# Latents and memory queries of an attention layer: from TensorE transposes to VectorE squares and transfers

## The reference, cut to what matters

```python
h = rmsnorm(x, pre_norm_g[l])
z = h @ w_in[l]
q_lat, kv_lat, k_pe, gb, gc, xin, q_mem, gate = split_cols(z)     # 512, 256, 64, ..., 512 columns
q = rmsnorm(q_lat, q_norm_g[l]) @ w_uq[l]                         # the latents, multiplied again
kv = rmsnorm(kv_lat, kv_norm_g[l]) @ w_ukv[l]
sc = einsum('bshd,bmhd->bhsm', q_mem, mk) * MEM_HEAD_DIM ** -0.5  # memory attention
```

## Time and profile before

| | us |
|---|---|
| median of three runs | 2298.61 |
| the profiled execution | 2298.59 |
| its span, first to last instruction | 2296.8 |
| PE busy | 2285.5 |
| DVE busy | 1506.8 |
| ACT busy | 1172.6 |

### The profile page before, as it was taken

The page is one execution under the profiler, slowest core; times in us unless marked ns, Lnnn a source line. Parts: engine busy times, 40 slices in busy tenths (PEclk is TensorE's granted clock), DMA queues, the critical chain, the costliest instruction groups (busy, mean ns, idle before and its releaser), DMA issues.

```text
span 2296.8 us, 27462 instructions
## 1 busy us (share of the span) xinstructions
PE 2285.5 (100%) x10741; PEld 1916.9 (83%) x10741; DVE 1506.8 (66%) x2067; ACT 1172.6 (51%) x1535; POOL 25.5 (1%) x35
## 2 busy tenths in 40 slices
PE   9999999999999999999999999999999999999998
PEld 7888888888888888888888888888888888888887
DVE  6677776756666666676466656675677856576764
ACT  6555655444445744444444444466555456556443
POOL 0000000000000000000000000000000000000000
PEclk9999999999999999999999999999999999999999
DMA  8666665766667566666666666666566665656664
GB/s 294 179 195 201 193 187 169 222 201 203 195 206 267 174 193 198 194 186 200 193 193 193 194 191 207 229 181 188 168 180 176 203 217 149 198 163 182 178 196 137
DMA packets 250129, 446.25 MB, mean 194 GB/s; under 512 B 20784, under 2 KB 55088, under 8 KB 249360
## 3 DMA queue, kind: packets, MB, share of 16 engines
q1 hardware_dynamic: 249568, 443.97, 63.7%
q10 hardware_dynamic: 432, 0.53, 0.1%
HBM read 434.99 MB, written 2.10 MB: 190 GB/s over the span
## 4 chain that ended last, share of the span: by engine, by line
PE 98%; DVE 1%; ACT 1%; DMA 0%; issue 0%; SPq 0%; DVEq 0%; ACTq 0%
PE pm L988 30%; PE pm L990 30%; PE pm L989 30%; PE pb L676 1%; PE pb L858 1%; PE pb L756 1%; DVE wl L2221 0%; PE pb L766 0%; DMA raw<-in_w_in 0%; ACT wh L1494 0%; PE pb L837 0%; PE pb L840 0%; PE pm L983 0%; PE pb L841 0%; PE pm L982 0%; PE pb L839 0%
## 5 line engine op out<-in xcount | busy, mean ns | idle before, releaser
L2221 DVE TENSOR_TENSOR wl<-raw,wh 128x1024 fp32r<-128x1024 f32 (+3 forms) x786 | 947.7, 1210 | 667.3 <-ACT wh L1494 664.0
L1494 ACT ACTIVATE wh<-raw 128x1024 fp32r<-128x1024 f32 (+3 forms) x786 | 819.2, 1046 | 901.3 <-PE pm L990 896.4
L988 PE MATMUL pm<-wh,hTh 128*128 128x512 f32 x702 | 275.2, 392 | 1.0 <-DVE wl L2221 1.0
L989 PE MATMUL pm<-wl,x2Th 128*128 128x512 f32 x704 | 273.9, 389 | 0.0
L990 PE MATMUL pm<-wh,x2Tl 128*128 128x512 f32 x704 | 273.9, 389 | 0.0
L988 PE MATMUL pm<-wh,x2Th 128*128 128x512 f32 x704 | 273.9, 389 | 0.0
L989 PE MATMUL pm<-wl,hTh 128*128 128x512 f32 x702 | 273.3, 389 | 0.0
L990 PE MATMUL pm<-wh,hTl 128*128 128x512 f32 x702 | 273.3, 389 | 0.0
L988 PE MATMUL pm<-wh,xT3h 128*128 128x512 f32 (+1 forms) x640 | 249.1, 389 | 0.0
L990 PE MATMUL pm<-wh,xT3l 128*128 128x512 f32 (+1 forms) x640 | 244.6, 382 | 0.0
L989 PE MATMUL pm<-wl,xT3h 128*128 128x512 f32 (+1 forms) x640 | 244.4, 382 | 0.0
(11 more groups left out here) (427 smaller groups left out, 3223.6 us busy)
## 6 DMA issues: line engine op xcount, KB each, us to landing
raw<-in_w_in SPq DMA_DIRECT2D x286, 512.0 KB, 3.9
raw<-in_w_ffn_gate SPq DMA_DIRECT2D x88, 512.0 KB, 4.3
raw<-in_w_ffn_up SPq DMA_DIRECT2D x88, 512.0 KB, 4.3
raw<-in_w_ffn_down SPq DMA_DIRECT2D x88, 512.0 KB, 4.1
raw<-in_w_o SPq DMA_DIRECT2D x64, 512.0 KB, 4.3
raw<-in_w_in SPq DMA_DIRECT2D x68, 256.0 KB, 3.5
raw<-in_w_branch_b SPq DMA_DIRECT2D x32, 512.0 KB, 4.2
raw<-in_w_out SPq DMA_DIRECT2D x32, 512.0 KB, 4.6
```

The source lines that it names most:

```text
L988: e.matmul(o, ah[:, kk, t], h[:, c], start=first, stop=False)
L989: e.matmul(o, ah[:, kk, t], l[:, c], start=False, stop=False)
L1494: e.activation(h[:, 0:n], r[:, 0:n], ACT.Copy).then_inc(s["hi"], 1)
L2221: e.tensor_tensor(l[:, 0:n], r[:, 0:n], h[:, 0:n].bitcast(F32), ALU.subtract).then_inc(s["lo"], 1)
```

## The change

The order of the first three groups becomes `qm`, `ql`, `kv`; the other groups keep their steps, and L is now the first step of `qm`. The 22 blocks that PE transposed in a layer (8 for `ql`, 4 for `kv`, 2 for the rope key, 8 for `qm`) are transposed as squares by DVE and moved by three batches of 16 transfers, as for `uq`. The two buffers, `latZ` and `latR`, are used by all three batches in turn; `kvZ` and `kvR` are the same memory. The results of round 4 are transposed into a buffer of their own, 12 steps earlier, and the level products of a head and what follows are due one step later.

```diff
+        add(f"qm{l}", "xT3", w_i, 2368, ev=("a", 2))
         add(f"ql{l}", "xT3", w_i, 0, ev=("a", 2))
         add(f"kv{l}", "xT3", w_i, 512, 320, ev=("a", 2))
-        add(f"qm{l}", "xT3", w_i, 2368, ev=("a", 2))
         gt(3)
         uq(0)
...
-RESULTS = ((1, 4, 12, 80, 100), (3, 4, 0, 135, 160), (4, 2, 4, 163, 173))
+RESULTS = ((1, 4, 12, 80, 100), (3, 4, 0, 135, 160), (4, 2, 4, 151, 163))
...
+            L = p.first[f"qm{l}"]
+            for i, (at0, free, value) in enumerate(((19, "c_l", 2 * l), (36, "qm_l", l + 1), (58, "ql_l", 4 * l + 4))):
+                Z, R = (m.kvZ, m.kvR[l]) if i == 2 else (m.latZ, m.latR[l])
+                for n in range(16):
+                    if n % 2 == 0:
+                        yield L + at0 + n // 2
+                    w.wait_ge(s["zl"], 4 * l + i + 1 + (i == 2))
+                    w.wait_ge(s[free], value)
+                    a_, c = n // 4, n % 4
+                    e.dma_start(R[32 * c:32 * c + 32, a_, :, :, :], Z[32 * a_:32 * a_ + 32, c, :, :, :]
+                                ).then_inc(s["d_lat"], 16)
...
-            yield at0 + 22 + i
+            yield at0 + 23 + i
...
-        yield from lat_turns(l, "ql", 2, L + 19)
-        yield from lat_turns(l, "kv", 1, L + 39)
-        yield L + 41
...
-            yield L + 50 + 2 * i
...
+    def latents(l):
...
+        yield p.first[f"qm{l}"] + 73
+        w.wait_ge(s["d_lat"], 768 * l + 768)
+        for k in range(2):
+            e.activation(m.kvT[0][:, k, :].rearrange("p (h a t) -> p h a t", h=2, a=4),
+                         m.kvR[l][:, :, k, :, :].rearrange("p a h t -> p h a t"), ACT.Copy, scale=m.gcol(f"kv{l}", k)
+                         ).then_inc(s["kv_h"], 1)
+        if l:
+            w.wait_ge(s["pv"], 12)
+        e.activation(m.kpeT[0][:, 0, :].rearrange("p (h a t) -> p h a t", h=2, a=4),
+                     m.kvR[l][:, :, 2, :, :].rearrange("p a h t -> p h a t"), ACT.Copy).then_inc(s["kp_c"], 1)
...
+        yield L + 34
+        w.wait_ge(s["d_lat"], 768 * l + 256)
+        e.activation(m.qmT[0][:, :, :].rearrange("p k (h a t) -> p k h a t", h=2, a=4),
+                     m.latR[l][:, :, :, :, :].rearrange("p a k h t -> p k h a t"), ACT.Copy).then_inc(s["qm_c"], 1)
+        yield L + 40
+        w.wait_ge(s["mk_c"], 2 * l + 2)
+        e.activation(m.mkS[0][:, :, :], m.mkT[l][:, :, :], ACT.Copy).then_inc(s["mk_h"], 1)
...
-        yield L + 37
+        yield L + 52
+        for k in range(4):
+            w.wait_ge(s["d_lat"], 768 * l + 512)
+            e.activation(m.qlT[0][:, k, :].rearrange("p (h a t) -> p h a t", h=2, a=4),
+                         m.latR[l][:, :, k, :, :].rearrange("p a h t -> p h a t"), ACT.Copy, scale=m.gcol(f"q{l}", k)
+                         ).then_inc(s["ql_h"], 1)
+        yield L + 54
         w.wait_ge(s["rstd"], RS[f"kv{l}"])
         for half in range(2):
             e.activation(m.S2[1][:, half, 0:256], m.S2[1][:, half, 0:256], ACT.Copy, scale=m.rs[f"kv{l}"][:, half:half + 1]
                          ).then_inc(s["kv_s"], 1)
-        yield L + 40
-        w.wait_ge(s["kv_t"], l + 1)
-        high_gain(6, m.kvT[0], 0, f"kv{l}", 0, "kv_h")
-        w.wait_ge(s["mk_c"], 2 * l + 2)
-        e.activation(m.mkS[0][:, :, :], m.mkT[l][:, :, :], ACT.Copy).then_inc(s["mk_h"], 1)
-        yield L + 42
-        w.wait_ge(s["kp_t"], l + 1)
-        if l:
-            w.wait_ge(s["pv"], 12)
-        e.activation(m.kpeT[0][:, :, :], view(7, 1), ACT.Copy).then_inc(s["kp_c"], 1)
-        yield p.end[f"qm{l}"]
-        w.wait_ge(s["ql_t"], 2 * l + 2)
-        w.wait_ge(s["sq"], SQ[f"ql{l}"])
-        taken(0, f"qm{l}", m.S2[0], scale=f"r{r}")
-        for i in range(2):
-            yield L + 51 + 2 * i
-            w.wait_ge(s["qm_t"], 2 * l + i + 1)
-            e.activation(m.qmT[0][:, 2 * i:2 * i + 2, :], view(6 + i), ACT.Copy).then_inc(s["qm_c"], 1)
...
+            for u in range(3):
+                r, n, k0, at0, split = RESULTS[u]
                 if u == 1:
                     yield from queries(l, (1, 2))
+                src, R = (m.yS4, m.yR4) if u == 2 else (m.yS, m.yR[l])
                 for i in range(16):
                     if u == 0 and i == 12:
                         yield from queries(l, (0,))
+                    if u == 2 and i == 8:
+                        yield from queries(l, (3,))
                     yield L + at0 + (i if n == 4 else i // 2)
                     w.wait_ge(s["ys"], 4 * (6 * l + r + 1))
-                    w.wait_ge(s["y_l"], 5 * l + u)
+                    w.wait_ge(s["y_l"], 5 * l + min(u, 1))
                     a, c = i // 4, i % 4
...
                 ins.then_inc(s["yq"], 1)
-                if u == 1:
-                    yield from queries(l, (3,))
-                yield L + split + 2
-                w.wait_ge(s["y_h"], 5 * l + (1, 2, 5)[u])
-                e.tensor_tensor(m.yT[1][:, k0:k0 + n, :], m.yR[l][:, 0:n, :], m.yT[0][:, k0:k0 + n, :].bitcast(F32),
-                                ALU.subtract).then_inc(s["y_l"], 1)
+                if u == 0:
+                    yield from results_low(l, 0)
+            yield from results_low(l, 1)
+            yield from results_low(l, 2)
...
-        w.wait_ge(s["kv_t"], l + 1)
+        w.wait_ge(s["d_lat"], 768 * l + 768)
...
+    def group_squares(S, n):
...
+        Z = m.latZ if n == 4 else m.kvZ
+        e.transpose(Z[:, :, 0:n, :, :].rearrange("p r k h t -> p k h r t"),
+                    S[:, :, 0:128 * n].rearrange("p h (k r c) -> p k h r c", k=n, r=4)).then_inc(s["zl"], 1)
+    def low_carried(dst, k, R, gname, after, value):
...
+        w.wait_ge(s["d_gain"], 16)
+        w.wait_ge(s[after], value)
+        for half in range(2):
+            hi, lo = (x[:, k, half * 128:half * 128 + 128].rearrange("p (a t) -> p a t", a=4) for x in dst)
+            ins = e.scalar_tensor_tensor(lo, R[:, :, k, half, :], m.gcol(gname, k), hi.bitcast(F32), ALU.mult, ALU.subtract)
+        return ins
...
     def layer(l):
-        L = p.first[f"ql{l}"]
+        L = p.first[f"qm{l}"]
+        yield p.end[f"qm{l}"] + 1
+        w.wait_ge(s["ev_a"], p.evac[f"qm{l}"])
+        w.wait_ge(s["xt_l"], 16 * l + 32)
+        group_squares(m.S2[0], 4)
         yield p.end[f"ql{l}"]
         variance(f"ql{l}", 512, SQ[f"ql{l}"], False)
-        for i in range(2):
-            yield L + 20 + i
-            low_gain(6 + i, m.qlT, 2 * i, f"q{l}", 2 * i, "ql_h", 4 * l + 2 * i + 2, "ql_l")
+        yield L + 34
+        w.wait_ge(s["ev_a"], p.evac[f"ql{l}"])
+        w.wait_ge(s["d_lat"], 768 * l + 256)
+        group_squares(m.S2[0], 4)
+        yield L + 35
+        w.wait_ge(s["qm_c"], l + 1)
+        hi, lo = (x[:, :, :].rearrange("p k (h a t) -> p k h a t", h=2, a=4) for x in m.qmT)
+        e.tensor_tensor(lo, m.latR[l][:, :, :, :, :].rearrange("p a k h t -> p k h a t"), hi.bitcast(F32), ALU.subtract
+                        ).then_inc(s["qm_l"], 1)
+        yield L + 42
+        w.wait_ge(s["mk_h"], l + 1)
+        e.tensor_tensor(m.mkS[1][:, :, :], m.mkT[l][:, :, :], m.mkS[0][:, :, :].bitcast(F32), ALU.subtract
+                        ).then_inc(s["mk_l"], 1)
         yield p.end[f"kv{l}"]
         variance(f"kv{l}", 256, SQ[f"kv{l}"], False)
...
-        yield L + 40
-        low_gain(6, m.kvT, 0, f"kv{l}", 0, "kv_h", 2 * l + 2, "kv_l")
-        w.wait_ge(s["mk_h"], l + 1)
-        e.tensor_tensor(m.mkS[1][:, :, :], m.mkT[l][:, :, :], m.mkS[0][:, :, :].bitcast(F32), ALU.subtract
-                        ).then_inc(s["mk_l"], 1)
-        yield L + 42
-        low(7, m.kpeT, 0, 1, "kp_c", l + 1, "kp_l")
-        for i in range(2):
-            yield L + 51 + 2 * i
-            low(6 + i, m.qmT, 2 * i, 2, "qm_c", 2 * l + i + 1, "qm_l")
+        yield L + 53
+        for k in range(4):
+            low_carried(m.qlT, k, m.latR[l], f"q{l}", "ql_h", 4 * l + k + 1).then_inc(s["ql_l"], 1)
+        yield L + 56
+        w.wait_ge(s["kv_s"], 2 * l + 2)
+        w.wait_ge(s["d_lat"], 768 * l + 512)
+        group_squares(m.S2[1][:, :, 0:256], 2)
+        w.wait_ge(s["rp"], RP[f"kv{l}"])
+        e.transpose(m.kvZ[:, :, 2, :, :].rearrange("p r h t -> p h r t"),
+                    m.kpd[:, :, :].rearrange("p h (r c) -> p h r c", c=32)).then_inc(s["zl"], 1)
```

More of the change, by code:

```diff
@@ L378, in buffers @@
     m.uqR = at("uqR", [128, 4, 3, 2, 32], RA + 16)
+    m.latZ = at("latZ", [128, 4, 4, 2, 32], RA)
+    m.kvZ = at("kvZ", [128, 4, 3, 2, 32], RA)
+    m.latR = [at(f"latR{l}", [128, 4, 4, 2, 32], (208, 200)[l]) for l in range(2)]
+    m.kvR = [at(f"kvR{l}", [128, 4, 3, 2, 32], (208, 200)[l]) for l in range(2)]
     m.kpeT = halves("kpeT", 1, 10.5, 218)
@@ L469, in ready @@
     r, ln = ((k - 12) // 2, k % 2) if k >= 12 else (2 + k // 2, k % 2)
-    return "y_l", 5 * layer + (r // 2 + 1 if r < 4 else 5 if r == 4 else 3 + ln)
+    return "y_l", 5 * layer + (r // 2 + 1 if r < 5 else 4 + ln)
 def sync_program(nc, s, m, a, cst, cpool, gains, out, p):
@@ L583, in background @@
```

(47 more changed lines are left out.)

30 lines of the change are left out of this document (17 added, 13 removed).

## The result

The changed kernel takes 2305.59 us (median of eight runs, 2303.91 to 2306.26) against 2298.52: 7.1 us more, ratio 1.0029, 95% interval 1.002 to 1.0039. I had forecast 2299.3 with a range to 2304.5. The profiled execution took 2305.48 us, its span is 2303.7: 6.9 more than before.

A forecast was written before the change was run, and what follows sets the result against it. The prediction took TensorE to bound the kernel (98% of the chain of waits). From 2298.59 us it took 7.4 for removed work and waits and added 8.1 for new waits: 2299.3, own range 2294 to 2303.5, over all cases 2291 to 2304.5.

The forecast's parts named there:

- the clock of the prediction: Time 0 is where PE crosses from `ql` into `kv`; batch 2 was forecast issued from 7.85 to 19.4 us.
- The landing of batch 2: Ahead of round 0: last two transfers issued at 19.4, landing 3.0 later at 22.4; bounds 1.8 and 4.1.
- The wait ahead of round 0: PE waits 2.2 us a layer ahead of the transposes of `P`, maxima 4.0 late; bounds 1.0 and 3.3.
- rival C: SP's queue: small transfers behind weight loads land after 4.7 instead of 3.0; 6.8 more, 2306.1 us; chance 0.15.
- Round 1: Batch 3 holds DVE 1.9 us in `uq_rope`; PE waits 1.0 a layer for `P`; bounds 0 to 2.1.
- Round 5: Twelve pieces of round 4 make the maxima 2.2 late; PE loses 0.85 a layer; bounds 0 and 1.3.
- the scores' 0.26 a layer: Round 5: second head's maxima and queries' low parts come later, 0 to 0.4 more, left to the range.
- transposes: 22 blocks a layer leave PE, 0.45 a four and 0.23 a pair: 5.0 us gained in two layers.
- level products: Third and fourth heads: due one step later, PE's waits for DVE's last `E` go; 1.35 us gained in all.
- `xi`: Ahead of the four of `xi`, PE's 0.54 wait for `yTl` goes: 1.1 us gained in two layers.
- Rival A: None of the late spots appears anywhere, only the gains of 7.4 remain: 2291.2 us; chance 0.2.

The follow-up runs named there:

- the last kernel: The change plus query-latent copies behind round 0, own batch 3 buffers, `uq_rope` waiting for batch 2, round 4's pieces in gaps: 2290.67 us; batch 3's copies at L+73/L+75: 2290.59.
- both tries of the gaps: The change with round 4's pieces moved into gaps: 2309.11 us; again with the third query's low parts back at L+155: 2302.62 us.

## Why the prediction was wrong

The places and the waits were right: PE idles for `P` in rounds 0 and 1 and for `PT` in round 5, and nowhere in `kv`. On the clock of the prediction (0 at 1584.37) batch 2 was issued from 7.83 (forecast 7.85) to 19.43 (19.4), and the maxima stood 9.1 behind the end of ACT's wait (9.3). Two steps failed: the landing and issue of batch 2 were taken too early, and idle time of TensorE was priced at its own length, with nothing for the granted clock.

1. **The landing of batch 2.** I took 3.0 for the last pair, from a median of 2.7. In the first layer it landed 4.5 after its issue, at 23.9, above the 4.1 that I had as the bound. In the second it was issued at 20.1, 0.7 later than forecast, landed 3.3 after that, at 23.4, and ACT waited 5.0. The wait ahead of round 0 became 3.4 us in the first layer (4.81 less 1.34 around the transposes, less 0.1 for the clock) and 2.5 in the second (idle 2.38 and the weight load), 1.5 more than the 4.4 forecast. This is rival C's mechanism, a queue behind a weight load, and I gave it 0.15; the run that puts the pair ahead of the load shows it for the first layer, 1.9 instead of 4.5, and hardly for the second, 3.0 instead of 3.3.
3. **Round 1**, 2.85 for 2.0: DVE's wait was 2.5, not 1.9, by the later issue and landing, and used up the same 0.9 to spare; the value product's 0.69 came with it.

4. **Round 5**, 2.17 for 1.7: the mechanism held (0.83 against 0.85), and the scores' 0.26 a layer, which I had left to the range, came.

The other terms: transposes 5.18 for 5.0, level products 1.52 for 1.35, `xi` 1.19 for 1.1. From 2299.3: + 3.2 (clock) + 1.5 (round 0's wait) + 0.85 + 0.69 (round 1) + 0.47 (round 5) + 0.19 (round 2) - 0.44 (gains) - 0.28 (ahead of the first slab) = 2305.5; profiled 2305.48.

Rival A, no late spot at all, is what the last kernel measures: 2291.2 forecast for it, 2290.67 and 2290.59 measured. The gain was real; the added waits, and the low clock that came with the longest of them, gave away twice as much.

## What to carry to other kernels

When a step waits for transfers, count what is queued behind the waiting instruction on its own engine, and put the reader where its queue has nothing urgent behind it: eight steps later cost nothing here and gave 9.3 us. Look at what stands ahead of the last transfer of a batch; one 512 KB load there added 2.6 us to a 1.9 us landing in the first layer, and only 0.3 in the second. Price long idle time of TensorE above its length: here 2.4 and 2.8 us of it came with losses of 4.1 and 5.1, while 1.1 us in the run with batch 2's last pair ahead of the load left the clock at 1.00.

## What the runs showed of the hardware

- Each idle time of TensorE of 2.30 to 2.78 us in these traces, ten in four kernels (the change, the squares of `uq0` without the wait, both tries of the gaps), had the granted clock at 0.50 for about 3 us behind it or from shortly before its end. In the run with a destination of its own for batch 2 an idle time of 1.45 did so in the first layer, and one of 1.62 in the second did not; behind 1.09 and 0.89 in other traces the clock stayed at 1.00. So the length of the idle time alone does not decide it; what does is open.
- A transfer of 32 partitions from SBUF to SBUF, the last of its batch, landed 1.9 us after its issue with five others ahead of it in the first layer, and 3.0 in the second. With a weight load close ahead it landed 4.5 and 3.3 after its issue, both times 0.3 behind the load (1607.94 and 1608.28; 1999.11 and 1999.42).
